# Experts' tokens fetched from DRAM by GpSimd's gathering DMA, in a two-layer decoder step

## The chip, the cores and the metric

One core of a Trainium2 chip. The metric is the device time of one execution in microseconds (us), the median of the runs. The core has five engines that run side by side, each with a queue of its own: TensorE (PE, its weight loads shown apart as PEld), VectorE (DVE), ScalarE (ACT), GpSimd (POOL) and SyncE (SP, which here only issues transfers). Sixteen DMA engines serve all queues. The engines meet at semaphores: an instruction counts one up, another engine waits for a value.

## The reference, cut

264 tokens (256 of a prompt, 8 of samples) pass two layers, the first with a gated-delta mixer and a dense SwiGLU, the second with block-sparse attention and eight expert SwiGLUs, of which each token uses two. What matters here is the last part:

```python
D_MODEL, D_FF, N_EXPERTS, TOP_K = 1024, 3584, 8, 2

def moe_swiglu(h, w_router, w_gate, w_up, w_down):
    logits = (h @ w_router).astype(jnp.float32)
    top_val, top_idx = lax.top_k(logits, TOP_K)
    wts = jax.nn.softmax(top_val, axis=-1)
    gates = jnp.sum(jax.nn.one_hot(top_idx, N_EXPERTS) * wts[..., None], axis=-2)
    y = jnp.zeros(h.shape, jnp.float32)
    for e in range(N_EXPERTS):
        y = y + gates[..., e:e + 1] * swiglu(h, w_gate[e], w_up[e], w_down[e])
    return y.astype(h.dtype)
```

## The kernel before

All is fp32. A product of fp32 precision is made of three matmuls in a faster format (fp32r): each operand is split into a high part, a rounded copy, and a low part, the rest, and hi x hi, hi x lo and lo x hi are added in a PSUM bank. Lines 953, 954 and 955 are these three in the experts, 128 x 512 each.

**Weights.** The experts come last and take more than half of the time. The weights of one expert are 42 pieces (`PIECES`) of 128 x 2048, 1 MB each: 28 for gate and up (`UP_PIECES`), 14 for down. SP loads them into a ring of 7 raw buffers, `raw_w` (L458). ScalarE writes the high part `w_hi` (L1213), VectorE subtracts it from the raw piece and writes `w_lo` (L1755), both into rings of 3 (`SPLIT`). A raw buffer is free when VectorE has subtracted (semaphore `split_lo`), and a place in `w_hi` and `w_lo` when TensorE has used the piece (`piece_used`). TensorE works 12 matmuls on a piece.

**Tokens.** An expert works on 128 slots (`CAP`), one for each of its tokens, empty ones at the end. `rpos` holds for every token and expert the number of its slot, or a negative number. `htok` holds the normed tokens, a token to a row, in three tiles of 128, 128 and 8 rows. For an expert VectorE makes `pick` (L1805), a matrix of ones and zeros, tokens by slots, and `pick_g` with the router's weights in place of the ones (L1803). TensorE's `gather` (L937) multiplies `htok` by `pick`, an fp32 product of 128 x 128 for each of 8 column blocks and 3 tiles, 24 in all. The result, the expert's tokens with the model dimension on the partitions, stands in banks 6 and 7. ScalarE takes it as `xe_hi` (L1234), VectorE as `xe_lo` (L1813), and these are the stationary operands of the expert's gate and up. The result of the expert is spread over the tokens with the turned `pick_g` (L947) and added to `xT` (L1819).

**Order.** Each engine's order is written out by hand, in a function `expert(v)` with a loop over the pieces `p`; the first expert is written once, the other seven are the body of a loop on each engine. On TensorE, after the matmuls of piece 24 `pick_g` is turned (L1000); every fourth piece from 8 to 32 is followed by four transposes of activations (L992); piece 38 is followed by `gather(v + 1)`, for the next expert. After the last expert this gathers once more, for an empty second round. On VectorE, `pick_tokens(v + 1)` stands behind the subtraction of piece 28, and `rest_of_gathered`, which writes `xe_lo`, behind that of piece 41; on ScalarE `take_gathered` stands at the same piece. Ahead of the experts TensorE counts positions (L923, L924, L926, semaphore `pos_ps`), VectorE makes `rpos` (from L1784) and the first picks, TensorE gathers for expert 0, and the experts begin. GpSimd has nothing to do between the store at L1341 and the last one at L1343. A second round of experts runs only if one has over 128 tokens (`over_cap`).

Of the kernel before, what the change touches and what calls it, by code (L numbers as in the profile page):

```python
# [29 lines left out]
P = 128  # L30
D = 1024
# [54 lines left out]
IN_PIECES = (QKV + H) * KT * P // PIECE  # L86

# [41 lines left out]
def program(nc, x_in, cst_in, lmask_in, rope_in, prm_in, conv_in, table_in, gdn_in_w, state_in, gdn_out_w,  # L129
            ffn_w, att_in_w, k_pages, v_pages, att_out_w, moe_w,  # L130
            y_out, convp_out, convs_out, deltap_out, deltas_out, kv_out):
    with ExitStack() as ctx:
# [35 lines left out]
        moe_scr = sb("moe_scr", [P, 7176])  # L168
        bank = [ctx.enter_context(nc.psum_tensor(f"bank{i}", [P, 512], F32))[:, :] for i in range(8)]
# [107 lines left out]
        def stat(rows, *dims):  # L277
# [25 lines left out]
        htok = carve(moe_scr, at, 3, D); at += 3 * D  # L303
        pick = carve(moe_scr, at, 3, CAP); at += 3 * CAP
# [22 lines left out]
        in_split_hi, in_split_lo = sem("in_split_hi"), sem("in_split_lo")  # L327
# [16 lines left out]
        f_split_hi, f_split_lo, f_used, f_silu, f_act, f_hi_set, f_lo_set, fh_hi_set, fh_lo_set, f_added = (  # L344
            sem(n) for n in ("f_split_hi", "f_split_lo", "f_used", "f_silu", "f_act", "f_hi_set", "f_lo_set", "fh_hi_set",
# [6 lines left out]
        pos_ps, over_set, h_turned, h_tok = sem("pos_ps"), sem("over_set"), sem("h_turned"), sem("h_tok")  # L352
        picked, gathered, ye_sb, spread_ps, spread_sb, comb, comb_added = (
# [16 lines left out]
        def slot_free(eng, n):  # L370

            m = n - SLOTS
            if C_AIN <= n < C_AIN + SLOTS:

                if n - C_AIN < F_RAW // 2:
                    eng.wait_ge(f_split_lo, PIECES - F_RAW + 2 * (n - C_AIN + 1))
                else:
                    eng.wait_ge(f_used, PIECES)
            elif n < C_OUT:
                eng.wait_ge(in_split_lo, IN_PIECES)  # L380
# [29 lines left out]
        def _(sp):  # L410
# [8 lines left out]
            for p in range(IN_PIECES):  # L419
                if p >= RAW:  # L420
                    sp.wait_ge(in_split_lo, p - RAW + 1)
# [7 lines left out]
            for p in range(PIECES):  # L429
                if p >= F_RAW:  # L430
                    sp.wait_ge(f_split_lo, p - F_RAW + 1)
# [41 lines left out]
        def _(pe):  # L473
# [42 lines left out]
            for c in range(QKV + H):  # L516
# [13 lines left out]
                if c % 2 == 0:  # L530
                    pe.wait_ge(in_split_lo, c // 2 + 1)
# [205 lines left out]
            def weight_tiles(p):  # L737
                pe.wait_ge(f_split_lo, p + 1)
# [180 lines left out]
            pe.wait_ge(r_gate, 1)  # L919
            for i, (t0, n) in enumerate(TOK_TILES):  # L920
# [19 lines left out]

            def combine(v, d):
# [15 lines left out]
            def expert(v, first=False):  # L957
                for p in range(PIECES):
                    pe.wait_ge(split_lo, v * PIECES + (p + 1))
# [35 lines left out]
                    if p == 24:  # L995
# [28 lines left out]
        def _(act):  # L1024
# [17 lines left out]
            def split_in(p):  # L1042
# [4 lines left out]
                A(w_hi[:, p % SPLIT, :], raw_w[:, p % RAW, :], ACT.Copy).then_inc(in_split_hi, 1)  # L1047
# [940 lines left out]
```

## Time and profile before

| what | us |
|---|---|
| median of 3 runs | 2016.27 (2015.77 to 2016.88) |
| the profiled execution | 2013.78 |
| its span, first to last instruction | 2012.0 |
| TensorE busy in the span | 1863.8 |
| VectorE busy | 1315.1 |
| ScalarE busy | 940.8 |
| GpSimd busy | 76.8 |

A page of the profile has the busy time of each engine, and the span in 40 equal slices (50.3 us each), with a digit for the busy tenths of an engine in each slice. Behind it stand views of the trace: windows (busy time of each engine in a stretch), waits (which engine waited for which, in total), timelines (instructions in order of time; equal ones that follow each other are merged, with their number behind an x), and the times of one line's instructions. Line numbers are those of the kernel before. TensorE's matmuls are pipelined, so the distance of two starts tells what one costs in a row of many, and the duration shown for one is longer than that.

### The profile page before, as it was taken

How to read it: one execution, taken by the hardware profiler on the slowest of the kernel's cores; microseconds unless marked ns; L12 is line 12 of the kernel's file. 1: busy time of each engine (PE TensorE's matmuls, PEld its weight loads, DVE VectorE, ACT ScalarE, POOL GpSimd, SP SyncE). 2: the span in 40 equal slices, each digit the busy share in tenths (PEclk: the TensorE clock that was granted, in tenths of full speed). 3: DMA queues.
4: the chain of work that ended last, by engine and by line, in shares of the span. 5: the costliest groups of instructions: out<-in, count | busy, mean ns of one | idle time of the engine just before them, and what ended most of it. 6: DMA issues, size and time to landing. Idle time of an engine off the chain costs nothing.

```text
span 2012.0 us, 27307 instructions
## 1 busy us (share of the span) xinstructions
PE 1863.8 (93%) x10177; PEld 1536.4 (76%) x10177; DVE 1315.1 (65%) x1359; ACT 940.8 (47%) x824; POOL 76.8 (4%) x94
## 2 busy tenths in 40 slices
PE   6999798899999973888999999999999999999996
PEld 4788783799998741366888888888888888888885
DVE  5863874454543231123887878879889788787894
ACT  3542000244431031012776767767677667676772
POOL 1340303000000000000000000000000000000000
PEclk8997795999999996796999999999999999999998
DMA  6222003355445789961998989989989899897980
GB/s 278 105 91 84 1 1 149 133 189 187 172 175 211 220 307 387 339 272 70 361 366 326 342 313 362 354 318 342 352 319 346 318 351 352 319 347 311 360 334 23
DMA packets 96731, 512.34 MB, mean 255 GB/s; under 512 B 10769, under 2 KB 10898, under 8 KB 44418
## 3 DMA queue, kind: packets, MB, share of 16 engines
q1 hardware_dynamic: 81936, 478.50, 63.2%
q10 hardware_dynamic: 13970, 25.46, 3.5%
q0 software_dynamic: 736, 7.21, 1.0%
q8 instruction: 54, 0.88, 0.2%
q14 instruction: 35, 0.29, 0.0%
HBM read 503.91 MB, written 7.21 MB: 254 GB/s over the span
## 4 chain that ended last, share of the span: by engine, by line
issue 65%; PE 28%; DVE 4%; ACT 1%; DMA 0%; SPq 0%; POOLq 0%; POOL 0%; ACTq 0%; DVEq 0%
PE bank L487 5%; PE bank L488 5%; PE bank L489 5%; PE bank L786 3%; PE bank L720 2%; PE bank L698 1%; PE bank L599 1%; PE bank L643 1%; PE bank L623 1%; PE bank L636 1%; DVE w_lo L1388 1%; PE bank L481 1%; ACT w_hi L1047 1%; DVE scr L1444 0%; PE bank L508 0%
## 5 line engine op out<-in xcount | busy, mean ns | idle before, releaser
L1755 DVE TENSOR_TENSOR w_lo<-raw_w,w_hi 128x2048 fp32r<-128x2048 f32 x336 | 768.6, 2290 | 140.7 <-ACT w_hi L1213 137.3
L1213 ACT ACTIVATE w_hi<-raw_w 128x2048 fp32r<-128x2048 f32 x336 | 644.9, 1920 | 369.6 <-PE bank L955 279.8
L953 PE MATMUL bank<-w_hi,xe_hi 128*128 128x512 f32 x896 | 365.1, 407 | 1.5 <-DVE xe_lo L1813 1.5
L955 PE MATMUL bank<-w_hi,xe_lo 128*128 128x512 f32 x896 | 350.5, 391 | 0.0
L954 PE MATMUL bank<-w_lo,xe_hi 128*128 128x512 f32 x896 | 349.9, 390 | 0.0
L488 PE MATMUL bank<-fh_lo,w_hi 128*128 128x264 f32 x704 | 201.6, 286 | 0.0
L953 PEld LDWEIGHTS bank<-w_hi,xe_hi 128*128 128x128 f32 x896 | 168.9, 189 | 35.9 <-issue 1.8
L955 PEld LDWEIGHTS bank<-w_hi,xe_lo 128*128 128x128 f32 x896 | 168.7, 188 | 36.2
L954 PEld LDWEIGHTS bank<-w_lo,xe_hi 128*128 128x128 f32 x896 | 168.9, 189 | 33.8
L953 PE MATMUL bank<-w_hi,aT_hi 128*128 128x512 f32 x448 | 176.9, 395 | 0.0
L954 PE MATMUL bank<-w_lo,aT_hi 128*128 128x512 f32 x448 | 174.5, 389 | 0.0
L955 PE MATMUL bank<-w_hi,aT_lo 128*128 128x512 f32 x448 | 174.4, 389 | 0.0
L1612 DVE TENSOR_TENSOR w_lo<-raw_w,w_hi 128x2048 fp32r<-128x2048 f32 x42 | 96.2, 2292 | 111.6 <-ACT w_hi L1127 111.6
L1127 ACT ACTIVATE w_hi<-raw_w 128x2048 fp32r<-128x2048 f32 x42 | 80.4, 1917 | 166.8 <-PE bank L489 123.2
L487 PE MATMUL bank<-f_hi,w_hi 128*128 128x264 f32 x480 | 141.1, 294 | 5.5 <-DVE w_lo L1388 5.5
L489 PE MATMUL bank<-f_hi,w_lo 128*128 128x264 f32 x480 | 137.2, 286 | 0.0
L488 PEld LDWEIGHTS bank<-fh_lo,w_hi 128*128 128x128 f32 x704 | 135.0, 192 | 0.0
L487 PE MATMUL bank<-fh_hi,w_hi 128*128 128x264 f32 x448 | 128.4, 287 | 5.8 <-DVE fh_lo L1383 5.8
L489 PE MATMUL bank<-fh_hi,w_lo 128*128 128x264 f32 x448 | 127.6, 285 | 0.0
L487 PEld LDWEIGHTS bank<-f_hi,w_hi 128*128 128x128 f32 x480 | 91.8, 191 | 14.2 <-DVE w_lo L1388 6.0
L953 PEld LDWEIGHTS bank<-w_hi,aT_hi 128*128 128x128 f32 x448 | 84.1, 188 | 18.7 <-DVE w_lo L1755 0.2
L955 PEld LDWEIGHTS bank<-w_hi,aT_lo 128*128 128x128 f32 x448 | 84.1, 188 | 17.8
(328 smaller groups left out, 2362.7 us busy)
## 6 DMA issues: line engine op xcount, KB each, us to landing
raw_w<-in_moe SPq DMA_DIRECT2D x336, 1024.0 KB, 4.8
raw_w<-in_ffn_w SPq DMA_DIRECT2D x42, 1024.0 KB, 4.8
ring<-in_k_pages SPq DMA_DIRECT2D x96, 256.0 KB, 3.5
raw_w<-in_gdn_in SPq DMA_DIRECT2D x16, 1024.0 KB, 5.4
ring<-in_v_pages SPq DMA_DIRECT2D x64, 256.0 KB, 11.6
ring<-in_v_pages ACTq DMA_DIRECT2D x64, 256.0 KB, 11.3
ring<-in_att_in SPq DMA_DIRECT2D x4, 2048.0 KB, 7.9
ring<-in_k_pages ACTq DMA_DIRECT2D x32, 256.0 KB, 7.5
```

The lines of the kernel that those rows point to most:

```text
L487: mm(out, hi, move_hi, start=first, stop=False)
L488: mm(out, hi, move_lo, start=False, stop=False)
L489: return mm(out, lo, move_hi, start=False, stop=last)
L720: last = mm(bank[4 + d % 4][:, 0:T], tile4(first + d // 4)[:, d % 4, h, :], src[:, h, :], start=(h == 0), stop=(h == H - 1))
L786: last = mm(bank[c % 4][:, 0:T], tile4(C_AIN + c // 4)[:, c % 4, k, :], hT[:, k, :], start=(k == 0), stop=(k == KT - 1))
L953: mm(out, hi, move_hi, start=first, stop=False)
L954: mm(out, hi, move_lo, start=False, stop=False)
L955: return mm(out, lo, move_hi, start=False, stop=last)
L1127: A(w_hi[:, p % SPLIT, :], raw_w[:, p % F_RAW, :], ACT.Copy).then_inc(f_split_hi, 1)
L1213: A(w_hi[:, p % SPLIT, :], raw_w[:, p % RAW, :], ACT.Copy).then_inc(split_hi, 1)
L1612: V.tensor_tensor(w_lo[:, p % SPLIT, :], raw_w[:, p % F_RAW, :], w_hi[:, p % SPLIT, :].bitcast(F32), ALU.subtract).then_inc(f_split_lo, 1)
L1755: V.tensor_tensor(w_lo[:, p % SPLIT, :], raw_w[:, p % RAW, :], w_hi[:, p % SPLIT, :].bitcast(F32), ALU.subtract).then_inc(split_lo, 1)
```

## The change

The first gather, for expert 0, stays as it was. For the others the product of tokens and picks goes, and three steps take its place.

1. Ahead of the experts TensorE adds one column to the count of positions (the triangular `upper` times ones: 1 for the first row, 128 for the last), VectorE makes of it `tok_no`, the tokens' numbers from 1 to 264 in three columns, and clears a row of `htok`. GpSimd stores the rows of `htok` in DRAM as rows 1 to 264 of `h_dram`, and the cleared one as row 0.
2. After piece 32 TensorE multiplies `pick` of the next expert by `tok_no` (`number_slots`): three fp32 products with one moving column, which give for each slot its token's number, or 0 for an empty slot. VectorE copies the column as integers to `slot_tok`, behind the subtraction of piece 34. GpSimd issues a DMA that gathers 128 rows of 4 KB from `h_dram` by these numbers into `x_slots`, which lies over the first tile of `htok`.
3. After piece 38 TensorE waits for the rows and turns them with eight transposes (`turn_slots`) into banks 6 and 7, where ScalarE and VectorE take them as before.

To have semaphores for this, the splits of the mixer's and the dense SwiGLU's weights count on the same pair as the experts' (`split_hi`, `split_lo`), and every wait on them has the earlier pieces added (`DENSE_PIECES`). `pick` is now made for all 128 rows of the third tile, since all of them are read.

```diff
 IN_PIECES = (QKV + H) * KT * P // PIECE
+DENSE_PIECES = IN_PIECES + PIECES
...
         moe_scr = sb("moe_scr", [P, 7176])
+        slot_tok = sb("slot_tok", [P, 1], I32)
+        tok_no = sb("tok_no", [P, 3])
+        h_dram = nc.dram_tensor("h_dram", [1 + T, D], F32, kind="Internal").ap()
         bank = [ctx.enter_context(nc.psum_tensor(f"bank{i}", [P, 512], F32))[:, :] for i in range(8)]
...
         htok = carve(moe_scr, at, 3, D); at += 3 * D
+        x_slots = htok[:, 0, :]
         pick = carve(moe_scr, at, 3, CAP); at += 3 * CAP
...
         pos_ps, over_set, h_turned, h_tok = sem("pos_ps"), sem("over_set"), sem("h_turned"), sem("h_tok")
+        slot_ps, slot_set, tok_rows = sem("slot_ps"), sem("slot_set"), sem("tok_rows")
         picked, gathered, ye_sb, spread_ps, spread_sb, comb, comb_added = (
...
                     if not first or p >= RAW:
-                        sp.wait_ge(split_lo, v * PIECES + (p - RAW + 1))
+                        sp.wait_ge(split_lo, v * PIECES + (DENSE_PIECES + p - RAW + 1))
                     else:
...
             pe.wait_ge(r_gate, 1)
+            mm(bank[0][:, 96:97], upper, ones[:, 0:1], start=True, stop=True)
             for i, (t0, n) in enumerate(TOK_TILES):
...
+            def number_slots(v):
+
+                pe.wait_ge(picked, v + 1)
+                for i in range(3):
+                    last = mm(bank[0][:, 0:1], pick[:, i, :], tok_no[:, i:i + 1], start=(i == 0), stop=(i == 2))
+                last.then_inc(slot_ps, 1)
+
+            def turn_slots(v):
+
+                pe.wait_ge(tok_rows, v * 16 + 64)
+                for half in range(2):
+                    for j in range(4):
+                        k = 4 * half + j
+                        last = nc.tensor.transpose(bank[6 + half][:, CAP * j:CAP * (j + 1)], x_slots[:, P * k:P * (k + 1)], ident)
+                    last.then_inc(gathered, 1)
+
             def combine(v, d):
...
                         last.then_inc(spread_ps, 1)
+                    if p == 32:
+                        number_slots(v + 1)
                     if p == 38:
                         pe.wait_ge(aT_lo_set, v * GROUPS + GROUPS)
-                        gather(v + 1)
+                        turn_slots(v + 1)
...
                     act.wait_ge(proj, 2 * (p - SPLIT + 1))
-                A(w_hi[:, p % SPLIT, :], raw_w[:, p % RAW, :], ACT.Copy).then_inc(in_split_hi, 1)
+                A(w_hi[:, p % SPLIT, :], raw_w[:, p % RAW, :], ACT.Copy).then_inc(split_hi, 1)
...
             pool.dma_start(kv_out, aq[:, 8:16, :]).then_inc(stored, 16)
+            pool.wait_ge(h_tok, 6)
+            pool.wait_ge(slot_set, 1)
+            for i, (t0, n) in enumerate(TOK_TILES):
+                pool.dma_start(h_dram[1 + t0:1 + t0 + n, :], htok[0:n, i, :]).then_inc(tok_rows, 16)
+            pool.dma_start(h_dram[0:1, :], htok[32:33, 2, :]).then_inc(tok_rows, 16)
+            pool.wait_ge(tok_rows, 64)
+
+            def fetch(v):
+
+                pool.wait_ge(slot_set, v + 1)
+                pool.wait_ge(gathered, v * 2)
+                G.indirect_dma_start(x_slots, None, h_dram, bass.IndirectOffsetOnAxis(ap=slot_tok[:, 0:1], axis=0))\
+                    .then_inc(tok_rows, 16)
+
+            for v in range(1, NE + 1):
+                fetch(v)
+            over_cap = pool.value_load(more[0:1, 0:1], min_val=0, max_val=1)
+            with pool.If(over_cap == 1):
+                for v in range(NE + 1, ROUNDS * NE + 1):
+                    fetch(v)
             pool.wait_ge(normed, 5 * KT)
...
             dve.wait_ge(pos_ps, 1)
+            V.memset(htok[32:33, 2, :], 0.0).then_inc(slot_set, 1)
+            for i in range(3):
+                V.tensor_scalar(tok_no[:, i:i + 1], bank[0][:, 96:97], float(P * i), None, ALU.add)
             link(V.memset(rpos, -1.0))
...
                                     ALU.is_equal, ALU.mult)
-                    last = V.tensor_scalar(pick[0:n, i, :], c_("slot_no")[0:n], rpos[0:n, i, at_v], None, ALU.is_equal)
+                    last = V.tensor_scalar(pick[:, i, :], c_("slot_no"), rpos[:, i, at_v], None, ALU.is_equal)
                 last.then_inc(picked, 1)
...
                         pick_tokens(v + 1)
+                    if p == 34:
+                        dve.wait_ge(slot_ps, v + 1)
+                        V.tensor_copy(slot_tok[:, :], bank[0][:, 0:1]).then_inc(slot_set, 1)
                     if p == PIECES - 1:
```

On TensorE, at the end of piece 32 of expert 0 (in the rows `moe_scr` is the memory that holds `htok`, `pick`, `pick_g` and the activations, and `cst` the constants, with the identity among them), before:

```order
3568 L955 MATMUL bank5<-w_hi,aT_lo 128x512
3569 L992 MATMUL bank6<-cst,moe_scr 128x128 x4
3570 L953 MATMUL bank4<-w_hi,aT_hi 128x512
3571 L954 MATMUL bank4<-w_lo,aT_hi 128x512
3572 L955 MATMUL bank4<-w_hi,aT_lo 128x512
```

and after:

```order
3569 L977 MATMUL bank5<-w_hi,aT_lo 128x512
3570 L1014 MATMUL bank6<-cst,moe_scr 128x128 x4
3571 L951 MATMUL bank0<-tok_no,moe_scr 128x1 x3
3572 L975 MATMUL bank4<-w_hi,aT_hi 128x512
3573 L976 MATMUL bank4<-w_lo,aT_hi 128x512
```

The three products into bank 0 stand directly behind the four transposes, ahead of piece 33.

On TensorE, at the end of piece 38 of expert 0, before:

```order
3641 L955 MATMUL bank5<-w_hi,aT_lo 128x512
3642 L937 MATMUL bank6<-moe_scr 128x128 x12
3643 L937 MATMUL bank7<-moe_scr 128x128 x12
3644 L953 MATMUL bank4<-w_hi,aT_hi 128x512
3645 L954 MATMUL bank4<-w_lo,aT_hi 128x512
```

and after:

```order
3643 L977 MATMUL bank5<-w_hi,aT_lo 128x512
3644 L960 MATMUL bank6<-cst,moe_scr 128x128 x4
3645 L960 MATMUL bank7<-cst,moe_scr 128x128 x4
3646 L975 MATMUL bank4<-w_hi,aT_hi 128x512
3647 L976 MATMUL bank4<-w_lo,aT_hi 128x512
```

Twenty-four products are now eight transposes, in the same place.

On VectorE, pieces 29 to 41 of expert 0 and the taking of the next tokens, after:

```order
632 L1799 TENSOR_TENSOR w_lo<-raw_w,w_hi 128x2048 x2
633 L1886 TENSOR_TENSOR aT_lo<-bank7,aT_hi 128x512
634 L1799 TENSOR_TENSOR w_lo<-raw_w,w_hi 128x2048 x2
635 L1895 CAST slot_tok<-bank0 128x1
636 L1799 TENSOR_TENSOR w_lo<-raw_w,w_hi 128x2048 x2
637 L1886 TENSOR_TENSOR aT_lo<-bank6,aT_hi 128x512
638 L1799 TENSOR_TENSOR w_lo<-raw_w,w_hi 128x2048 x5
639 L1860 TENSOR_TENSOR xe_lo<-bank6,xe_hi 128x512
```

The copy of the slots' numbers, which waits for TensorE, stands between the subtractions of pieces 34 and 35; nothing else moved.

On GpSimd, its last instructions, after:

```order
73 L1365 DMA out_kv<-scr 128x2112
74 L1369 DMA h_dram<-moe_scr 128x1024 x2
75 L1369 DMA h_dram<-moe_scr 8x1024
76 L1370 DMA h_dram<-moe_scr 16x1x64
77 L1377 DMA moe_scr<-h_dram,slot_tok 128x1024 x8
78 L1382 TENSOR_LOAD more
```

Before, the last store (`out_y`) followed the one of `out_kv` directly; now the four stores of the rows and eight gathers stand between them.

## Rows read from the trace of the kernel before

**Rows 1.** Page, 40 slices: TensorE's busy tenths, granted clock, DMA share.

```profile
PE   6999798899999973888999999999999999999996
...
PEclk8997795999999996796999999999999999999998
DMA  6222003355445789961998989989989899897980
```

**Rows 2.** Windows: busy PE, PEld, DVE, ACT, POOL; clock, DMA share, GB/s.

```profile
1000.00:1100.00 100.00, 100.00 (x463) 82.07 (x462) 82.33 (x52) 68.42 (x46) 0.00 (x0) 1.00 0.90 344
...
1600.00:1700.00 100.00, 100.00 (x456) 82.58 (x455) 89.45 (x63) 72.11 (x49) 0.00 (x0) 1.00 0.92 355
```

**Rows 3.** Waits, 950 to 1950 us: who for whom, total us, times, longest.

```profile
ACT w_hi L1213 <- PE bank L955: 273.5, 297, 6.3
DVE w_lo L1755 <- ACT w_hi L1213: 133.2, 217, 7.6
...
PEld bank L953 <- DVE w_lo L1755: 0.6, 2, 0.4
```

**Rows 4.** Timeline of TensorE at two gathers: start, duration, instruction.

```profile
1056.24 8.40 PE L937 MATMUL bank<-moe_scr 128*128 128x128 f32 x48
...
1186.48 0.39 PE L955 MATMUL bank<-w_hi,aT_lo 128*128 128x512 f32 x1
1186.71 8.40 PE L937 MATMUL bank<-moe_scr 128*128 128x128 f32 x48
...
1195.38 0.40 PE L954 MATMUL bank<-w_lo,aT_hi 128*128 128x512 f32 x1
```

**Rows 5.** Timeline of TensorE at four transposes.

```profile
970.38 0.39 PE L955 MATMUL bank<-w_hi,xe_lo 128*128 128x512 f32 x1
970.61 0.60 PE L992 MATMUL bank<-cst,moe_scr 128*128 128x128 f32 x4
...
971.28 0.39 PE L954 MATMUL bank<-w_lo,xe_hi 128*128 128x512 f32 x1
```

**Rows 6.** Timeline of TensorE at the count of positions.

```profile
922.39 0.33 PE L924 MATMUL bank<-small,cst 128*128 128x8 f32 x2
922.57 0.37 PE L923 MATMUL bank<-small,cst 128*128 128x8 f32 x2
```

**Rows 7.** Timeline of VectorE after the count.

```profile
923.85 0.12 DVE L1784 MEMSET small<- 128x75 f32 x1 [1.58 <-PE bank L926]
...
924.65 0.16 DVE L1792 COPY small<-small 128x24 f32<-128x24 f32 x1
924.73 0.16 DVE L1791 TENSOR_SCALAR small<-small 128x24 f32<-128x24 f32 x1
```

**Rows 8.** Timelines of VectorE and TensorE behind piece 32.

```profile
1169.37 2.29 DVE L1755 TENSOR_TENSOR w_lo<-raw_w,w_hi 128x2048 fp32r<-128x2048 f32 x1 [0.35 <-ACT w_hi L1213]
1172.09 2.29 DVE L1755 TENSOR_TENSOR w_lo<-raw_w,w_hi 128x2048 fp32r<-128x2048 f32 x1 [0.43 <-ACT w_hi L1213]
...
1169.94 0.60 PE L992 MATMUL bank<-cst,moe_scr 128*128 128x128 f32 x4
```

**Rows 9.** DMAs: KB each, median us to landing; one issue of GpSimd.

```profile
raw_w<-in_moe SPq DMA_DIRECT2D x336, 1024.0 KB, 4.8
...
out_kv<-scr POOLq DMA_DIRECT2D x1, 1056.0 KB, 7.2
...
out_deltap<-ring POOLq DMA_DIRECT2D x1, 512.0 KB, 13.1
...
130.35 1.53 POOL L1314 DMA_DIRECT2D out_convs<-conv_new  x1
```

**Rows 10.** Timeline of ScalarE: splitting piece 41, taking half of the tokens.

```profile
1186.91 1.91 ACT L1213 ACTIVATE w_hi<-raw_w 128x2048 fp32r<-128x2048 f32 x1 [0.80 <-PE bank L955]
1190.93 0.60 ACT L1234 ACTIVATE xe_hi<-bank 128x512 fp32r<-128x512 f32 x1 [2.11 <-PE bank L937]
```

**Rows 11.** Window ahead of a gather: TensorE busy, clock, DMA share, GB/s.

```profile
1180.00:1190.00 10.00, 10.00 (x51) 1.00 1.00 390
```

More of the change, by code:

```diff
@@ L343, in program @@
         outp, out_added = sem("outp"), sem("out_added")
-        f_split_hi, f_split_lo, f_used, f_silu, f_act, f_hi_set, f_lo_set, fh_hi_set, fh_lo_set, f_added = (
-            sem(n) for n in ("f_split_hi", "f_split_lo", "f_used", "f_silu", "f_act", "f_hi_set", "f_lo_set", "fh_hi_set",
+        f_used, f_silu, f_act, f_hi_set, f_lo_set, fh_hi_set, fh_lo_set, f_added = (
+            sem(n) for n in ("f_used", "f_silu", "f_act", "f_hi_set", "f_lo_set", "fh_hi_set",
                              "fh_lo_set", "f_added"))
@@ L375, in slot_free @@
                 if n - C_AIN < F_RAW // 2:
-                    eng.wait_ge(f_split_lo, PIECES - F_RAW + 2 * (n - C_AIN + 1))
+                    eng.wait_ge(split_lo, IN_PIECES + PIECES - F_RAW + 2 * (n - C_AIN + 1))
                 else:
@@ L379, in slot_free @@
             elif n < C_OUT:
-                eng.wait_ge(in_split_lo, IN_PIECES)
+                eng.wait_ge(split_lo, IN_PIECES)
             elif n < C_AIN:
@@ L420, in _ @@
                 if p >= RAW:
-                    sp.wait_ge(in_split_lo, p - RAW + 1)
+                    sp.wait_ge(split_lo, p - RAW + 1)
                 sp.dma_start(raw_w[:, p % RAW, :], gdn_in_w[p]).then_inc(piece_full[p % RAW], 16)
@@ L430, in _ @@
                 if p >= F_RAW:
-                    sp.wait_ge(f_split_lo, p - F_RAW + 1)
+                    sp.wait_ge(split_lo, IN_PIECES + p - F_RAW + 1)
                 elif p < 4:
@@ L530, in _ @@
                 if c % 2 == 0:
-                    pe.wait_ge(in_split_lo, c // 2 + 1)
+                    pe.wait_ge(split_lo, c // 2 + 1)
                 if c >= 4:
@@ L958, in expert @@
                 for p in range(PIECES):
-                    pe.wait_ge(split_lo, v * PIECES + (p + 1))
+                    pe.wait_ge(split_lo, v * PIECES + (DENSE_PIECES + p + 1))
                     buf = p % SPLIT
@@ L1126, in split_f @@
                     act.wait_ge(f_used, p - SPLIT + 1)
-                A(w_hi[:, p % SPLIT, :], raw_w[:, p % F_RAW, :], ACT.Copy).then_inc(f_split_hi, 1)
+                A(w_hi[:, p % SPLIT, :], raw_w[:, p % F_RAW, :], ACT.Copy).then_inc(split_hi, 1)
             act.wait_ge(outp, KT)
@@ L1385, in rest_of_in @@
             def rest_of_in(p):
-                dve.wait_ge(in_split_hi, p + 1)
+                dve.wait_ge(split_hi, p + 1)
                 V.tensor_tensor(w_lo[:, p % SPLIT, :], raw_w[:, p % RAW, :], w_hi[:, p % SPLIT, :].bitcast(F32),
-                                ALU.subtract).then_inc(in_split_lo, 1)
+                                ALU.subtract).then_inc(split_lo, 1)
             dve.wait_ge(small_ready, 1)
@@ L1609, in rest_of_piece @@
             def rest_of_piece(p):
-                dve.wait_ge(f_split_hi, p + 1)
+                dve.wait_ge(split_hi, IN_PIECES + p + 1)
                 V.tensor_tensor(w_lo[:, p % SPLIT, :], raw_w[:, p % F_RAW, :], w_hi[:, p % SPLIT, :].bitcast(F32),
-                                ALU.subtract).then_inc(f_split_lo, 1)
+                                ALU.subtract).then_inc(split_lo, 1)
             rest_of_piece(0)
```

5 lines of the change are left out of this document (2 added, 3 removed).

## The prediction

> **What bounds the kernel now.** I read the slices of the page first: from the twentieth to the thirty-ninth, that is through the experts, TensorE's digit is 9 and the DMA engines' 8 or 9 [rows 1]. So one of the two sets the pace. The windows decide it: in 100 us stretches inside the experts TensorE is busy 100.00 of 100.00 us at a granted clock of 1.00, VectorE 82 to 89 us, ScalarE 68 to 72 us, and the DMA share is 0.90 to 0.92 [rows 2]. The table of waits says who waits for whom between 950 and 1950 us: ScalarE waits 273.5 us for TensorE's matmuls to give back a `w_hi` buffer, VectorE 133.2 us for ScalarE, and TensorE's weight loads wait 0.6 us for VectorE in all [rows 3]. The weights' DMAs wait for slots as well, and land 4.8 us after issue at the median [rows 9]. Everything waits for TensorE, and TensorE for nobody. So each microsecond of work that leaves TensorE's queue in the expert loop leaves the span, until another engine or the DMA comes due.
>
> One expert lasts from one gather to the next, 1186.71 - 1056.24 = 130.47 us [rows 4]. It holds 42 pieces of 12 matmuls.
>
> **What leaves TensorE.** The gather of the next expert's tokens is 24 fp32 products, shown as 48 records in 8.40 us. What it costs in the queue is the distance of its neighbours: the matmul before it starts at 1186.48, the second one behind it at 1195.38, 8.90 us apart, where plain matmuls follow each other at 0.23 us (1186.48 to 1186.71), 0.227 over a long row, so 0.45 for two. The gather costs 8.90 - 0.45 = 8.45 us [rows 4], or 0.352 us for each product. It stands at piece 38 of every expert, the last included: eight times. The first gather, ahead of expert 0, stays.
>
> **What comes to TensorE.** (a) Eight transposes of 128x128 at piece 38. The same form stands in the trace, in fours: 970.38 to 971.28 is 0.90 us, less 0.45 for two plain steps is 0.45 us a four [rows 5]. Two of them: 0.90 us. (b) At piece 32 three fp32 products with 128 columns of weights and one moving column. The trace has no such operation. From above: three of the gather's, 3 x 0.352 = 1.06 us. Nearest is the count of positions ahead of expert 0, with the same weights and eight moving columns, which start at 922.39 and 922.57 [rows 6], near 0.2 us each, so 0.60 us for three, and that with the clock at 0.6 of full speed in that slice [rows 1]; half of it, 0.30 us, is the lower end. I take 0.70 us, the nearest row and a little for the wait ahead of it. Sum for one expert: 8.45 - 0.90 - 0.70 = 6.85 us (ends 6.49 and 7.25). Eight times: 54.8 us (51.9 to 58.0).
>
> **What is added ahead of expert 0.** Here TensorE waits for VectorE's picks, so all of it is on the path: one more small product (0.20 us by rows 6), a memset of 1x1024 and three 128x1 operations on VectorE. Small operations of this chain follow each other at 0.08 us to 0.18 us, and a memset of 75 columns takes 0.12 us [rows 7]; 0.3 us for the three. For the memset the upper end is VectorE's streaming rate, 2.29 us for 2048 columns [rows 8], so 1.15 us for 1024; the lower is 0.12 us. I take 0.8 us, nearer the rate. Sum 1.3 us (0.6 to 1.65). Writing the 264 rows to DRAM, 1.08 MB from GpSimd's queue, lies beside the first gather, where the DMA engines are nearly idle, and nobody needs the rows for more than 100 us: nothing. GpSimd has no other work there. The renamed semaphores carry the same counts, and the address sums that SP gains are hidden, since its transfers wait for slots: nothing.
>
> **Where the gathering DMA hides.** Its window: the three products end piece 32's extras, some 0.45 + 0.70 us behind the start of the transposes at 1169.94, at 1171.1 and no later than 1171.5. VectorE is then in the subtraction of piece 34, which ends at 1169.37 + 2.29 = 1171.66 [rows 8]; the new copy of the numbers takes the 0.43 us gap ahead of the next subtraction, at 1172.09, so VectorE loses nothing and what is queued behind the wait is not late. The numbers are there at about 1171.9. TensorE wants the rows at the end of piece 38, 1186.71 [rows 4] and 0.7 us more for the new products: 1187.4. The window is 15.5 us long. What a gather of 128 rows of 4 KB takes, the trace does not show. Direct DMAs on the same queue land after 7.2 us (1056 KB) and 13.1 us (512 KB, issued right behind one of 4096 KB on its own queue); the longest issue takes 1.53 us [rows 9]. I take 8 us, near the first, because the weights stream beside it and the issue has to read 128 numbers. The window covers it with 7 us to spare; nor can it cost less than nothing, since TensorE asks for the rows only at piece 38. If that cover is gone, each further us costs 8 us in all, since every expert waits once.
>
> The Trainium skill, "SBUF — State Buffer", section "Who interferes with whom", says that a VectorE instruction with two SBUF inputs keeps out a GpSimd instruction that reads SBUF for its whole length. VectorE's subtraction is such an instruction, so by that rule the reading of the numbers may wait; no row of before shows whether it does, and it is rival 3 below.
>
> **What is late next.** Behind the gather's place ScalarE splits piece 41, takes both halves of the new tokens (1.91 us and twice 0.60 us [rows 10]) and splits piece 0 of the next expert; until now it had 8.45 us of standing still for that. Counted from the end of piece 38: ScalarE is done with piece 41 at 2.1, with the halves at 3.3, starts piece 0 when piece 39 is used, 0.90 + 2.72 = 3.6, and ends at 5.7; VectorE subtracts by 8.1 (2.29 us). TensorE wants it at 0.90 + 3 x 2.72 = 9.1. Slack 1.0 us: no wait.
>
> **The sum.** 54.8 - 1.3 = 53.5 us off. The profiled execution took 2013.78 us with a span of 2012.0, so 1960.3 us there; the median of the runs is 2016.27 us, 2.5 us above it, and the forecast is **1962.8 us**, its own range 1959 to 1966 by the ends above.
>
> **Rival 1, the DMA engines' rate becomes the bound.** One expert moves 42 x 1.0486 = 44.04 MB, and the gather adds 0.52 MB. In 130.47 us that is 338 GB/s today; in 123.6 us it is 360 GB/s. The best 100 us stretch moved 355 GB/s [rows 2]. If that were the ceiling, an expert would last 44.56 MB / 355 GB/s = 125.5 us, 1.9 us more than TensorE wants, 15 us in all: 1978 us. Against it: that stretch was held back by TensorE, and the 10 us ahead of a gather moved 390 GB/s with the share at 1.00 [rows 11], which would do an expert in 114 us. For it: at share 1.00 nothing is left, and the gather's pause, in which the transfers caught up, is gone. I give it 1 in 10. The Trainium skill, "DMA: Bandwidth & Descriptors", section "Where 436 GB/s comes from", puts the HBM's side at about 358 GB/s per core; by that an expert would take 124.5 us and the kernel some 7 us more than forecast. The 390 GB/s disagrees with it over 10 us.
>
> **Rival 2, the rows come somewhat late.** The landing goes as the third DMA of rows 9 did, 13.1 us, and issue or reading adds 3 to 5 us: 16 to 18 us against 15.5. TensorE stands 1 to 3 us an expert, 8 to 24 us in all, 1971 to 1987 us. 1 in 10.
>
> **Rival 3, the change costs time.** VectorE subtracts 2.29 us out of every 2.72 and stands 0.43 [rows 8], 16% of the time. If GpSimd's work for the gather only went on in these gaps, 2.5 us of it would take 15.6 us; with 7.2 us to land that is 22.8 us, 7.3 us late, 58 us in all, against 53.5 saved: 2021 us. It decides from 22.2 us on (15.5 + 53.5 / 8). With the 1.53 us of the longest issue in rows 9 it would be 9.6 + 7.2 = 16.8 us, rival 2's size. A TensorE that stands so long may also lose its clock: in the nineteenth slice, where it waits for the picks ahead of expert 0, the granted clock is 0.6 [rows 1]; that would come on top. 8 in 100.
>
> **Rival 4, the change does nothing for time**: transposes and products cost as much as the gather did. That would take 8.45 / 11 = 0.77 us for each of the eleven, where rows 5 show 0.11: 2016 us. 2 in 100.
>
> **How the numbers follow.** Forecast 0.70, rival 1 0.10, rival 2 0.10, rival 3 0.08, rival 4 0.02. The range takes the forecast's low end and a little for the unknown products, 1958, and reaches up over rival 1 and the nearer part of rival 2, to 1985: it leaves out some 0.15. About 0.2% is what a measurement of this kernel can tell from no change; faster by over that 0.90 (forecast, rivals 1 and 2), within it 0.02, slower 0.08.
>
> **What would show it.** The distance between two turnings should be 123.6 us. The record of three products should cost 0.3 to 1.1 us, the transposes 0.9 us. TensorE's busy time in the 100 us windows should stay at 100; if not, the wait ahead of the transposes names the gather (rivals 2, 3) or a weight load names VectorE, and behind it a DMA (rival 1). The gather's time to landing should be under 15.5 us. The forecast fails if that time is longer, if the weights' time to landing grows from 4.8 us beyond some 12 us, or if VectorE's subtraction grows beyond 2.29 us beside GpSimd's work.

## The result and the profile after

| what | before | after |
|---|---|---|
| median of the runs, us | 2016.02 | 1961.74 (1959.15 to 1964.31) |
| ratio | | 0.9732, 95% interval 0.9715 to 0.9748 |
| span of the profiled execution, us | 2012.0 | 1957.5 |
| one expert, us | 130.47 | 123.60 |
| first matmul of expert 0 at, us | 943.37 | 944.28 |

Run again later, beside the kernel before and three of the kernels below, the changed kernel took 0.9747 (0.9731 to 0.9764). The forecast was 1962.8 us.

The page's slices after; the first row answers to [rows 1] and is as full as it was, the DMA share is now 9 throughout the experts.

```profile
PE   6999798899999985677999999999999999999996
...
PEclk8998796899999999787899999999999999999998
DMA  7222002455554879993499999999999999999991
```

Windows inside the experts (length, then busy us and instructions of PE, PEld, DVE, ACT, POOL; granted clock, DMA share, GB/s), to be laid beside [rows 2]:

```profile
1100.00:1200.00 100.00, 100.00 (x461) 82.76 (x460) 88.54 (x60) 72.50 (x51) 0.96 (x1) 1.00 0.94 359
...
1600.00:1700.00 100.00, 100.00 (x459) 82.71 (x458) 88.22 (x61) 72.82 (x51) 0.94 (x1) 1.00 0.94 362
```

TensorE still has no idle time, and its clock is still 1.00. In the mean of the 100 us windows inside the experts VectorE went from 84 to 89 us, since the same work now stands in a shorter expert, and the transfers went from 339 to 359 GB/s. The waits between 950 and 1900 us, beside [rows 3]:

```profile
POOL moe_scr L1377 <- DVE slot_tok L1895: 848.8, 7, 122.7
ACT w_hi L1237 <- PE bank L977: 266.4, 297, 5.5
DVE w_lo L1799 <- ACT w_hi L1237: 111.7, 210, 6.7
...
PEld bank L975 <- DVE w_lo L1799: 0.6, 2, 0.4
```

The new row is GpSimd waiting for its numbers, which costs nobody anything. No row has TensorE waiting for the gathering DMA. Now TensorE's timeline, at the turning of the rows in two experts and at the numbers' products of the second (L975 to L977 are the matmuls on the weights, L1014 the transposes of activations, L951 the numbers' products, L960 the turning):

```profile
1057.05 1.04 PE L960 MATMUL bank<-cst,moe_scr 128*128 128x128 f32 x8
...
1162.96 0.39 PE L977 MATMUL bank<-w_hi,aT_lo 128*128 128x512 f32 x1
1163.19 0.60 PE L1014 MATMUL bank<-cst,moe_scr 128*128 128x128 f32 x4
1163.62 0.73 PE L951 MATMUL bank<-tok_no,moe_scr 128*128 128x1 f32 x6
...
1164.53 0.39 PE L976 MATMUL bank<-w_lo,aT_hi 128*128 128x512 f32 x1
...
1180.42 0.39 PE L977 MATMUL bank<-w_hi,aT_lo 128*128 128x512 f32 x1
1180.65 1.04 PE L960 MATMUL bank<-cst,moe_scr 128*128 128x128 f32 x8
...
1181.75 0.40 PE L976 MATMUL bank<-w_lo,aT_hi 128*128 128x512 f32 x1
```

From one turning to the next, 1057.05 to 1180.65, is 123.60 us. By the way of counting of [rows 4] the eight transposes cost 1181.75 - 1180.42 - 0.45 = 0.88 us, the four transposes and the three products 1164.53 - 1162.96 - 0.45 = 1.12 us, and the products alone 1.12 - 0.45 = 0.67 us. VectorE's and GpSimd's timelines at the copy of the numbers, and the times of the gathering DMA from its own line (of eight: shortest, median, longest):

```profile
1162.62 2.29 DVE L1799 TENSOR_TENSOR w_lo<-raw_w,w_hi 128x2048 fp32r<-128x2048 f32 x1 [0.35 <-ACT w_hi L1237]
1164.83 0.15 DVE L1895 CAST slot_tok<-bank 128x1 int32<-128x1 f32 x1
1165.33 2.29 DVE L1799 TENSOR_TENSOR w_lo<-raw_w,w_hi 128x2048 fp32r<-128x2048 f32 x1 [0.35 <-ACT w_hi L1237]
...
1165.25 0.96 POOL L1377 DMA_INDIRECT moe_scr<-h_dram,slot_tok  x1 [120.25 <-DVE slot_tok L1895]
...
DMA to landing us min/median/max: 6.1/7.2/9.8
```

The DMA is issued at 1165.25, TensorE asks for the rows at 1180.65, a window of 15.4 us, and rows land 6.1 to 9.8 us after issue. The longest landing is that of the first gather, whose window is shorter. Timelines of VectorE and GpSimd there:

```profile
1041.29 0.15 DVE L1895 CAST slot_tok<-bank 128x1 int32<-128x1 f32 x1
1041.79 2.29 DVE L1799 TENSOR_TENSOR w_lo<-raw_w,w_hi 128x2048 fp32r<-128x2048 f32 x1 [0.35 <-ACT w_hi L1237]
1042.27 2.73 POOL L1377 DMA_INDIRECT moe_scr<-h_dram,slot_tok  x1 [115.21 <-DVE slot_tok L1895]
```

It is issued at 1042.27 and asked for at 1057.05, 14.8 us later, so 5.0 us are to spare there; the other seven have 5.8 us or more. This one issue also takes 2.73 us where the others take 0.93 to 0.96 us. It begins 0.47 us behind the start of a subtraction, and it ends, at 1045.00, 0.9 us behind the end of that subtraction.

Ahead of expert 0, VectorE's timeline, beside [rows 7]:

```profile
923.44 0.91 DVE L1828 MEMSET moe_scr<- 1x1024 f32 x1 [3.09 <-PE bank L932]
924.38 0.29 DVE L1830 TENSOR_SCALAR tok_no<-bank 128x1 f32<-128x1 f32 x3
924.63 0.12 DVE L1831 MEMSET small<- 128x75 f32 x1
```

What stood at the start of this row of operations now comes 1.2 us later. From TensorE's last count of positions to the first matmul of expert 0 it took 19.97 us before and takes 21.49 us now. The product that the change adds on TensorE stands ahead of that count, so it is not in this difference. It lies in the stretch from VectorE's last step on the router's weights to the last count. Its two ends, from the timelines of before and then of after, and a window in it (columns as above), in the same order:

```profile
922.09 0.18 DVE L1781 TENSOR_TENSOR small<-small,scr 128x24 f32<-128x24 f32 x1
923.40 0.37 PE L926 MATMUL bank<-small,cst 128*1 128x8 f32 x6
920.16 0.19 DVE L1825 TENSOR_TENSOR small<-small,scr 128x24 f32<-128x24 f32 x1
922.79 0.37 PE L932 MATMUL bank<-small,cst 128*1 128x8 f32 x6
922.00:924.00 2.00, 1.77 (x22) 1.42 (x22) 0.36 (x3) 0.95 (x2) 0.00 (x0) 1.00 0.80 262
922.00:924.00 2.00, 1.17 (x15) 0.91 (x15) 0.56 (x1) 0.00 (x0) 0.00 (x0) 0.50 0.72 303
```

That is 1.31 us before and 2.63 us after. Most of the difference is the clock, which was 1.00 there in the one execution and 0.50 in the other. The first, third and sixth kernels below have the added product and a clock of 1.00 there, and take 1.53 to 1.54 us, so the product itself costs some 0.2 us.

### The profile page after: what moved, and what is told of

Same layout as the page of the kernel before. It is cut to its first block, busy times and chain, and to the rows that moved or that the text cites. A ratio compares the mean times of both kernels' runs of the same rounds, so it can differ in the third digit from the quotient of the medians.

```text
span 1957.5 us, 27112 instructions
## 1 busy us (share of the span) xinstructions
PE 1807.6 (92%) x9907; PEld 1496.2 (76%) x9907; DVE 1315.8 (67%) x1371; ACT 938.8 (48%) x824; POOL 88.2 (5%) x106
## 4 chain that ended last, share of the span: by engine, by line
PE 78%; issue 9%; DVE 6%; ACT 2%; ACTq 2%; SPq 1%; DMA 1%; POOLq 0%; POOL 0%; DVEq 0%
PE bank L975 14%; PE bank L977 14%; PE bank L976 14%; PE bank L492 5%; PE bank L493 5%; PE bank L494 5%; PE bank L725 3%; PE bank L791 3%; PE bank L703 1%; PE bank L604 1%; PE bank L648 1%; PE bank L969 1%; PE bank L1014 1%; PE bank L628 1%; ACTq L405 1%
## 5 line engine op out<-in xcount | busy, mean ns | idle before, releaser
L975 PE MATMUL bank<-w_hi,xe_hi 128*128 128x512 f32 x896 | 364.9, 407 | 1.5 <-DVE xe_lo L1860 1.5
L977 PE MATMUL bank<-w_hi,xe_lo 128*128 128x512 f32 x896 | 350.1, 391 | 0.0
L977 PEld LDWEIGHTS bank<-w_hi,xe_lo 128*128 128x128 f32 x896 | 168.5, 188 | 36.1
L975 PEld LDWEIGHTS bank<-w_hi,xe_hi 128*128 128x128 f32 x896 | 168.6, 188 | 35.9 <-issue 1.8
L975 PE MATMUL bank<-w_hi,aT_hi 128*128 128x512 f32 x448 | 176.7, 394 | 0.0
L977 PE MATMUL bank<-w_hi,aT_lo 128*128 128x512 f32 x448 | 174.7, 390 | 0.0
L975 PEld LDWEIGHTS bank<-w_hi,aT_hi 128*128 128x128 f32 x448 | 84.1, 188 | 17.8 <-DVE w_lo L1799 0.2
L977 PEld LDWEIGHTS bank<-w_hi,aT_lo 128*128 128x128 f32 x448 | 84.1, 188 | 17.7
## 6 DMA issues: line engine op xcount, KB each, us to landing
ring<-in_v_pages SPq DMA_DIRECT2D x64, 256.0 KB, 11.3
```

Source lines behind the costliest of these rows:

```text
L975: mm(out, hi, move_hi, start=first, stop=False)
L977: return mm(out, lo, move_hi, start=False, stop=last)
```

## The experiments

Two theories stood at the start. The first: TensorE's queue alone sets the time in the experts, what leaves it counts in full, and the gather's DMA is hidden with some 7 us of cover. The second: the transfers' rate is, or is about to be, the bound, so that part of the gain goes to it. The distance between the first matmuls of two experts was read from each trace beside the whole time. From the second expert on it repeats within 0.05 us where nothing makes TensorE wait; the first expert starts at a low clock and is left out of this figure.

**1. No gathering DMA.** GpSimd's loop of fetches goes, and the wait ahead of the transposes is for the stored rows only. So all experts but the first work on the first 128 tokens as they lie, not on their own.

```diff
-                pe.wait_ge(tok_rows, v * 16 + 64)
+                pe.wait_ge(tok_rows, 64)
...
-            for v in range(1, NE + 1):
-                fetch(v)
```

> Leaves the gathering DMA out: TensorE makes the slots' numbers and turns the first 128 tokens of htok as they lie, without a wait for rows. Theory (TensorE's queue sets the time and the gather's DMA is hidden): as the changed kernel, 1961.7 us, within 2 us. Rival (the transfers' rate is the bound, and the 8 x 0.52 MB take their share of it): 4.2 MB less at some 360 GB/s, up to 12 us less, near 1950 us.

Measured: 0.9751 (0.9735 to 0.9768) of the kernel before, against 0.9732 and 0.9747 for the changed kernel. One expert: 123.60 us, as with the DMA. The gathering DMA costs nothing that can be seen; the 12 us of the second theory are not there.

**2. The numbers beside the old gather.**

```diff
-                        turn_slots(v + 1)
+                        gather(v + 1)
...
-            for v in range(1, NE + 1):
-                fetch(v)
```

> One part of the change alone: the numbers' products, their copy, tok_no and the store of the rows are there, but no gathering DMA, and the next expert's tokens come from the 24 products as before. Theory (every product in TensorE's queue counts in full): 2016.0 + 8 x 0.66 us + some 1.5 us ahead of the experts = 2022.8 us. Rival (the numbers' products slip into slack beside weight loads): 2017.5 us.

Measured: 2024.86 us, 1.0065 (1.0042 to 1.0088), so some 11 to 13 us more than before instead of 7. The trace has it in parts: an expert lasts 131.16 us, 0.69 us more than 130.47, in eight experts 5.5 us. From the count to expert 0 it is 21.49 us instead of 19.97, 1.5 us. These two are as expected. The rest of the 11.3 us between the spans is of other kinds. Up to the count it is 1.8 us, of which 1.3 us lie in the stretch with the added product, which took 2.63 us at a clock of 0.50 as in the trace after. Behind the last expert it is some 3.6 us, most of it a pause of 2.69 us between two of TensorE's last sums, which the trace of before does not have and for which the profile shows no reason. Against it, expert 0 had 1.1 us less of the low clock in it. The theory holds for what was edited; the total says less than it seems.

**3 and 4. The gather later.** The products and their copy go to later pieces, nothing else.

```diff
-                    if p == 32:
+                    if p == 35:
                         number_slots(v + 1)
...
-                    if p == 34:
+                    if p == 37:
                         dve.wait_ge(slot_ps, v + 1)
```

(36 and 38 in the second.)

> The numbers' products move from piece 32 to piece 35, their copy from piece 34 to 37, so the gather is issued three pieces (8.2 us) later. Its median landing after 7.2 us leaves 7.3 us of cover in the changed kernel, 4.7 us for the first expert's, which lands after 9.8 us. Theory (the cover is the window less the landing): late by 0.9 us in seven experts and 3.5 us in the first, 1962 + 9 = 1971 us, between 1962 and 1975. Rival (the landing is short when not beside many transfers, or the wait costs more than its length): 1962 us or over 1980 us.

> The numbers' products at piece 36, their copy at piece 38, so the gather is issued four pieces (10.9 us) later. Theory: late by 3.6 us in seven experts and 6.2 us in the first, 31 us in all: 1993 us, and the wait ahead of the transposes names the DMA. Rival (a TensorE that stands loses its clock too, and more than the lateness): over 2005 us, with a granted clock under 1.00 behind the waits.

Measured: 1976.74 us, 0.9827 (0.9808 to 0.9846), and 1996.83 us, 0.9905 (0.9871 to 0.9939); that is some 15 to 19 us and 32 to 35 us over the changed kernel. So the cover is real and ends where it was computed to end. The first was expected at 1971 us, at most 1975; the landings, 6.0 to 10.0 us for all but the last gather, explain most of the miss, since the expectation took the median for seven of them. In the first, with 6.7 us from issue to asking, the experts whose gather lands after 6.0 and 6.7 us still last 123.6 to 123.7 us, and those with 8.4 and 9.2 us last 125.5 and 126.2 us. One with 8.7 us lasts 127.35 us, more than it was late. The second kernel shows why. TensorE's timeline and windows around the end of one wait:

```profile
1198.37 0.39 PE L977 MATMUL bank<-w_hi,aT_lo 128*128 128x512 f32 x1
1203.34 1.97 PE L960 MATMUL bank<-cst,moe_scr 128*128 128x128 f32 x8 [4.58 <-DMA moe_scr<-h_dram,slot_tok]
1204.96 0.77 PE L975 MATMUL bank<-w_hi,aT_hi 128*128 128x512 f32 x1
1205.54 0.63 PE L976 MATMUL bank<-w_lo,aT_hi 128*128 128x512 f32 x1
...
1200.00:1202.90 2.90, 0.00 (x0) 0.00 (x0) 2.48 (x2) 0.71 (x1) 0.00 (x0) 1.00 1.03 428
1202.90:1206.30 3.40, 2.96 (x11) 2.76 (x12) 1.15 (x3) 1.20 (x2) 0.00 (x0) 0.50 1.01 414
1206.30:1210.00 3.70, 3.70 (x17) 3.00 (x16) 0.37 (x1) 1.38 (x1) 0.00 (x0) 1.00 0.69 290
```

The rows were issued at 1194.53 and landed 8.8 us later, and TensorE began 0.04 us after that. It had stood 4.6 us, and was then granted 0.50 of its clock for 3.4 us: the eight transposes show 1.97 us instead of 1.04. From the second expert on, one whose rows were late without such a drop lasts 0.1 to 0.2 us more than TensorE was late; with the drop it is 1.6 to 1.7 us more. It came after three of the seven waits that held TensorE up here, and after two of four in the other kernel. So both readings of the fourth expectation were partly right: the lateness is the larger part, the clock the smaller. Counted from the first matmul of expert 0 to the end, the first kernel took 13.8 us more than the changed kernel for 10.5 us of standing late, the second 30.9 us for 25.7 us.

**5 and 6. More rows beside the weights.** Behind each gather, three or seven more blocks, into a tile that nothing reads any more (here with three).

```diff
             for v in range(1, NE + 1):
                 fetch(v)
+                for i in range(3):
+                    if v > 1 or i:
+                        pool.wait_ge(more_rows, 16 * (3 * (v - 1) + i))
+                    pool.dma_start(htok[:, 1, :], h_dram[1:1 + P, :]).then_inc(more_rows, 16)
```

> Behind each gather GpSimd loads three more blocks of 128 rows of 4 KB from the stored tokens into a tile that nothing reads any more: 1.57 MB more for each expert, 373 GB/s in the mean at an expert of 123.6 us. Theory (the DMA engines have room, up to some 400 GB/s, and the ring of seven pieces takes 4 us of backlog): no change, 1961.7 us within 2 us. Rival (a ceiling near 360 GB/s): 46.1 MB / 360 GB/s = 128.2 us an expert, 37 us more, 1998 us.

> The same with seven more blocks, 3.67 MB more for each expert, 390 GB/s in the mean. Theory (a ceiling near 400 GB/s, a ring that holds 10 us of cover): 9 us of backlog right behind the gather, so at or just over the edge: 1962 to 1985 us. Rival (a ceiling near 360 GB/s): 48.2 MB / 360 GB/s = 134 us an expert, 83 us more, 2044 us.

Measured: 0.9748 (0.9734 to 0.9763) and 0.9746 (0.9730 to 0.9761), one expert 123.60 us in both. No time was lost that can be seen, even with eight times the rows. Windows of the kernel with seven blocks more, two long ones and one right behind a gather:

```profile
1200.00:1300.00 100.00, 100.00 (x459) 82.68 (x458) 88.81 (x64) 70.78 (x48) 3.70 (x6) 1.00 0.98 385
1300.00:1400.00 100.00, 100.00 (x457) 82.68 (x456) 88.37 (x61) 72.96 (x51) 2.69 (x5) 1.00 0.98 393
...
1205.00:1215.00 10.00, 10.00 (x46) 8.26 (x45) 8.76 (x6) 7.60 (x5) 0.54 (x1) 1.00 1.02 423
...
raw_w<-in_moe SPq DMA_DIRECT2D x306, 1024.0 KB, 6.8
```

The engines moved 393 GB/s over 100 us and 423 GB/s over 10 us. The weights then landed after 6.8 us at the median instead of 4.8, and the ring took it. A ceiling of 355 to 360 GB/s is excluded for a core that runs alone, as here. The Trainium skill has both answers: in "Where 436 GB/s comes from" of "DMA: Bandwidth & Descriptors" about 358 GB/s binds a core's transfers from memory, while "Specifications (TRN2)" of "HBM Reference" lets a core that streams alone go well above that share. Here one core runs, and the trace agrees with the second.

**7. The first expert's tokens by DMA too.** The row of zeros is cleared ahead of the wait for positions, and the counts of the semaphores move by one gather.

```diff
-            gather(0)
+            number_slots(0)
+            turn_slots(0)
             expert(0, first=True)
...
             pick_tokens(0)
+            dve.wait_ge(slot_ps, 1)
+            V.tensor_copy(slot_tok[:, :], bank[0][:, 0:1]).then_inc(slot_set, 1)
             rest_of_gathered(0)
```

> The first expert's tokens come by the gathering DMA as well, in place of the 24 products that TensorE makes at its lower clock in 15.03 us. The zero row is cleared ahead of the wait for positions. Theory (here nothing hides the DMA): numbers and copy 1.5 us, first issue 2.7 us with a landing of 9.8 us, transposes 1.8 us, some 13 us against 15 us, 0 to 3 us faster than the changed kernel, unless TensorE's clock rises later for its standing still: 1959 to 1964 us. Rival (the rows' store, 3.6 us, and the gather follow each other on the path and TensorE starts the expert later): 1965 to 1970 us.

> The kernel that fetches the first expert's tokens too, once more beside the changed kernel. Theory (from the count of positions to the first expert's first matmul it takes 14.1 us where the changed kernel takes 21.5 us): 5 to 7 us faster than the changed kernel, 0.970 of the kernel before. Rival (the difference of the first time was jitter ahead of the experts): the same as the changed kernel within 2 us.

Measured: 1956.54 us, 0.9712 (0.9693 to 0.9732), and again 1957.61 us, 0.9710 (0.9694 to 0.9726), beside 0.9747 for the changed kernel in the same company. TensorE's timeline of the first run, from the last count on:

```profile
927.60 0.37 PE L932 MATMUL bank<-small,cst 128*1 128x8 f32 x6
931.28 1.41 PE L951 MATMUL bank<-tok_no,moe_scr 128*128 128x1 f32 x6 [3.31 <-DVE moe_scr L1854]
938.25 1.97 PE L960 MATMUL bank<-cst,moe_scr 128*128 128x128 f32 x8 [5.56 <-DMA moe_scr<-h_dram,slot_tok]
941.72 0.76 PE L975 MATMUL bank<-w_hi,xe_hi 128*128 128x512 f32 x1 [1.50 <-DVE xe_lo L1862]
```

927.60 to 941.72 is 14.1 us instead of 21.5. Of these 7.4 us 1.3 come from clearing the row of zeros earlier, since the wait ahead of TensorE's first product here is 3.31 us instead of 4.58; the other 6.1 us are the gather's. Here nothing hides the DMA, and it still gains, for two reasons: the products stood at TensorE's low clock and took 15.03 us, and with the DMA engines quiet the gather landed after 4.5 us instead of 6 to 10. I had expected 0 to 3 us, with a landing of 9.8 us.

**8. The additions off the path.** The zeros are cleared ahead of the wait for positions, TensorE's product goes behind the count and into bank 1, and `tok_no` is made behind the first picks.

```diff
+            V.memset(htok[32:33, 2, :], 0.0).then_inc(slot_set, 1)
             dve.wait_ge(pos_ps, 1)
-            V.memset(htok[32:33, 2, :], 0.0).then_inc(slot_set, 1)
-            for i in range(3):
-                V.tensor_scalar(tok_no[:, i:i + 1], bank[0][:, 96:97], float(P * i), None, ALU.add)
```

> What the change adds ahead of expert 0 is taken off the path: the row of zeros is cleared while VectorE waits for the positions, the tokens' numbers are made behind the first picks, and TensorE's product for them stands behind the count. Theory (this work is on the path there, 1.5 us): 1960.2 us, TensorE's wait for the first picks back from 4.58 to 3.1 us. Rival (it was beside other work): 1961.7 us and the same wait.

Measured: 1960.61 us, 0.9732 (0.9718 to 0.9746), which does not tell it from the changed kernel. In the trace the way from the count to expert 0 is 19.99 us instead of 21.49, and TensorE's wait for the picks 2.77 us instead of 4.58. So these 1.5 us were on the path. The median is 1.1 and 2.4 us under the two medians of the changed kernel, which fits, but it is no more than the stages ahead of the count move by: the profiled execution, the slowest of five, reached the count only at 930.85 us, the changed kernel at 922.79.

**9. The changed kernel again.**

> The changed kernel once more, beside the next three on the same chip. Every theory: 0.973 of the kernel before, experts of 123.60 us; what differs from the first time shows how far the stages ahead of the experts move by themselves.

Measured: 1962.98 us, 0.9747 (0.9731 to 0.9764), experts of 123.60 us, 21.49 us from the count to expert 0.

**10 and 11. TensorE kept busy while it waits.** On top of the seventh experiment; the result of these matmuls is never read. The tenth kernel has 8 in the wait for the picks and 14 in the wait for the rows, the eleventh 12 and 22, and 26 more ahead of the router. A wait for the first split piece of weights, which they read, stands ahead of them.

```diff
+            def keep_warm(n, ready=None):
+                for _ in range(n):
+                    mm(bank[2][:, 0:N], w_hi[:, 0, 0:P], w_hi[:, 0, 0:N], start=True, stop=True)
...
             last.then_inc(pos_ps, 1)
+            keep_warm(8)
...
             number_slots(0)
+            keep_warm(14)
             turn_slots(0)
```

> The kernel that fetches the first expert's tokens too, with 8 matmuls of 512 columns whose result nobody reads while TensorE waits for the first picks, and 14 while it waits for the rows. Theory (TensorE's low clock at the start of expert 0 comes from its standing still): the clock is back at 1.00 when expert 0 starts, its first nine matmuls take 0.23 instead of 0.43 us, the transposes half: 2 to 3 us less, 0.969. Rival (they delay what is waited for, or the clock stays low): the same or up to 2 us more.

> The same with 26 such matmuls ahead of the router, while TensorE waits 7.4 us for the normed tokens, 12 in the wait for the picks and 22 in the wait for the rows. Theory (kept busy, TensorE stays at its high clock through the router, whose 48 records take 7.48 us at the low one): 4 to 7 us less than the kernel without them, 0.967. Rival (the router's products are bound by something else, or the clock falls in spite of them and the matmuls overshoot): as the one with fewer, or slower.

Measured: 1955.34 us, 0.9698 (0.9682 to 0.9714), and 1951.74 us, 0.9688 (0.9672 to 0.9704). From TensorE's timeline of the second, L718 being the filling and L916 the router's products:

```profile
902.58 6.21 PE L718 MATMUL bank<-w_hi 128*128 128x512 f32 x26
909.99 4.61 PE L916 MATMUL bank<-prm,hT 128*128 128x8 f32 x48 [1.20 <-DVE hT L1422]
...
928.36 5.26 PE L718 MATMUL bank<-w_hi 128*128 128x512 f32 x22
933.79 1.09 PE L967 MATMUL bank<-cst,moe_scr 128*128 128x128 f32 x8 [0.16 <-DMA moe_scr<-h_dram,slot_tok]
936.55 0.47 PE L982 MATMUL bank<-w_hi,xe_hi 128*128 128x512 f32 x1 [1.67 <-DVE xe_lo L1870]
```

The 48 records of the router's products take 4.61 us instead of 7.48, and the turning 1.09 instead of 1.97. The clock fell again soon after expert 0 began, from 937.1 to 940.5, and with fewer matmuls its first ones ran low as well, so the expectation of a high clock at that point failed while the direction of the time held. The intervals of the two and of the seventh (0.9694 to 0.9726) overlap one another, so the gain of the filling over the seventh kernel rests on the traces: in the eleventh's the router's products take 2.9 us less and the way from the count to expert 0 is 13.6 us instead of 14.1. The kernel with 26, 12 and 22 has the lowest median, and its whole interval lies under that of the changed kernel, by near 0.6% in the middle.

## Why the prediction was right

- **What bounds.** TensorE, before and after: 100.00 of 100.00 us in every window inside the experts. Right.
- **What leaves and what comes.** 8.45 us for the gather; transposes 0.90 forecast, 0.88 measured; products 0.70 and 0.67. One expert 6.85 forecast, 130.47 - 123.60 = 6.87 measured. The product of one moving column costs 0.22 us each, near the row of eight columns and far under the gather's 0.352, so the choice by the nearest row was the good one. The text had read that row as one at a clock of 0.6, which is the mean of its slice; the window from 922 to 924 us shows 1.00, so the row needed no halving and the low end of 0.30 us had no ground.
- **Ahead of expert 0.** 1.3 us forecast, of which 0.2 for the product ahead of the count. Behind the count 21.49 - 19.97 = 1.52 us were measured instead of 1.1, and with the product's 0.2 us it is 1.7 to 1.8 us, just over the upper end of 1.65. The memset took 0.91 us where 0.8 was taken, the rest a little more as well. Between the two profiled executions the whole way grew by 2.8 us, 1.1 of them because the count ran at the other clock; the forecast had no term for that. The eighth experiment shows that the work behind the count lies on the path, and that clearing a row could have been put into VectorE's wait.
- **Where the DMA hides.** The window was 15.5 us forecast, 15.4 measured, 14.8 for the first gather. The landing of 8 us stood for 6.1 to 9.8, median 7.2. Experiments 3 and 4 show that the cover ends at that distance; the price was more than the 8 us for each us late, because of the clock, which the text had only as an addition to rival 3.
- **What is late next.** Slack 1.0 us forecast. VectorE ended the subtraction of piece 0 at 1186.43 + 2.29 = 1188.72 in the trace after, and TensorE loaded it at 1189.73: 1.0 us. The text's own terms, 3.6 and 1.91, give 5.5 us for the end of ScalarE's split and not 5.7, so 1.3 us of slack; ScalarE in fact began at 3.8.
- **Rival 1** was wrong by a good distance: 360 GB/s is what the kernel asks for, and eight times the rows, 389 GB/s in the mean from 1100 to 1900 us, cost nothing. The 10 us row at 390 GB/s was the better witness than the 100 us one, which TensorE held back.
- **Rivals 2 and 3** did not come about. Of rival 3, though, the traces show a part that stayed hidden. Seven times, each time at the first gather of a kernel, the issue began some 0.5 us inside a subtraction of VectorE. It then took 2.66 to 2.74 us, and each time it ended 0.91 us behind that subtraction's end: 2.73 us where 1.82 us of it were left, 2.66 us where 1.75 us were. The other gathers beside the weights begin 0.01 to 0.09 us ahead of a subtraction and take 0.93 to 0.99 us, with the subtraction running all through, and with VectorE idle the first of the seventh experiment takes 1.05 us. By these rows an issue that comes inside a subtraction stands until its end, some 1.8 us here. One that comes just ahead of it does not wait, and the making of the transfers goes on beside the subtraction, not in the gaps alone. That is what the rule of "Who interferes with whom" in "SBUF — State Buffer" of the Trainium skill would have of an issue that has to read its numbers, and these traces agree with it. No run moved the issue on purpose to try it.
- **The sum.** 53.5 us forecast, 54.28 between the medians and 54.44 between the spans (2011.98 and 1957.54). Between the profiled executions: seven distances between experts' first matmuls give 48.86 us (7.66 for expert 0, which had less of the low clock in it, and 6.85 to 6.90 for the others), the last expert and what follows 6.49, together 55.35; less 1.52 behind the count and 1.32 in the stretch ahead of it, plus 1.93 by which this execution was earlier at the start of that stretch: 54.44. That the total came so near the forecast is partly luck, since the stages ahead of the experts move by some us from execution to execution.

## What to carry to other kernels

Where one engine never idles, price an edit by the distance between its neighbours in that engine's queue, not by busy time, and check it after by a distance that repeats, such as one turn of a loop. A product with a matrix of ones and zeros that only picks rows can be replaced by a DMA that picks them, if the numbers are ready well ahead; the cover has to hold the slowest landing, and moving the issue by a few steps in either direction measures it. When work on the path is at a low clock, even a DMA that nothing hides can be the shorter way.

## What the runs showed of the hardware

- A gather of 128 rows of 4 KB landed 4.1 to 4.5 us after issue with few other transfers in flight, and 5.9 to 10.2 us beside the weights. Issuing took 0.93 to 0.99 us, and 1.05 us for the first one of the seventh experiment. It took 2.66 to 2.74 us where it began inside a subtraction of VectorE with two inputs in SBUF, and ended 0.91 us behind it, in seven traces of seven. Long idleness of GpSimd is not the cause: later gathers with over 120 us of it took 0.93 to 0.96 us.
- The sixteen DMA engines of one core that runs alone held 393 GB/s over 100 us, and 423 GB/s over 10 us.
- TensorE's granted clock went from 1.00 to 0.50 for 3.4 us around the end of waits of 1.9, 3.9, 4.2 and 4.6 us for the rows, and for 6.8 us around that of one of 6.6 us. It did not after others of 1.6, 1.8, 2.3, 2.4, 2.4 and 2.7 us. Which waits are followed by it stays open; the length of the wait alone does not say.
- The last count of positions began between 922.8 and 932.4 us in executions of kernels that differ by 0.2 us ahead of it, leaving out the one with matmuls ahead of the router. The count itself ran at a clock of 1.00 in some of them and 0.50 in others, which made 1.1 us. The rest of the cause was not looked for.
